# A second kernel's tail woven with gathers: 1.8 instead of 1.2 rows' weight for a turn of attention, 1.0 instead of 1.1 elsewhere, and the small diagonals made on VectorE

## The chip, the cores and the metric

One core of a Trainium2 chip runs the whole program. The metric is the device time in microseconds of one execution, as the median of three runs. The engines are TensorE (PE; its weight loads are PEld), VectorE (DVE), ScalarE (ACT), GpSimd (POOL) and SyncE (SP), which issues the loads of the weights.

## The reference

Two blocks work on 512 tokens of 1024 channels in fp32. The first ends in a mixture of 16384 experts: every token takes 8 x 16 = 128 of them, each with a row `u` and a row `v` of 1024 numbers.

```
ue = take(expert_u, expert);  ve = take(expert_v, expert)
h  = gelu(einsum('thkd,td->thk', ue, xc))
out = einsum('thk,thkd->td', gate * h, ve)
```

The second block is attention with 8 heads (two softmaxes a head, "diff"), an MLP of width 4096 with squared relu, a second attention with 8 heads ("mla"), a second MLP, and a norm. Both attentions are causal, so the first 256 tokens can pass through the whole second block before the last 256 are known.

## The kernel before

**The rows.** An expert's `u` and `v` lie together (8 KB). What the code calls row `n` is one of 512 gathers: GpSimd issues an indirect DMA that brings 128 experts' pairs, one to a partition, 1 MB in all (L1754). VectorE multiplies the `u` half with the token and sums (the dot, L1892), ScalarE makes the gelu (L1847), multiplies it with the gate (L1849) and makes a diagonal matrix of the 128 results (L1856 or L1859), and TensorE adds diagonal times `v` into PSUM (L1778 or L1782). Rows 0 to 255 belong to tokens 0 to 255. From row 256 on a row is "stacked": it holds 32 experts for each of four tokens, its diagonal is 128x32 (`each32` is four 32x32 identities), and its product is 4 matmuls. The rows lie in a ring: 6 buffers from row 236 and 7 from row 278 on. GpSimd issues the gather of row n when TensorE is done with row n-7.

**The tail.** From row 256 on, the second block for tokens 0 to 255 (`halves[0]`) runs with the remaining rows. Each engine's program is written as generators that yield once a turn; `beside` adds `rate * weight` for each yield and takes one step of the row generator whenever the sum passes 1. The same turns are counted on PE, ACT and DVE, so their orders agree. A turn in a projection or an MLP's first product is 24 matmuls of 128x256 (weight 1), in an MLP's second product 12 (weight 0.5). A turn of attention (19 turns for the 16 blocks of 128 queries, since it is pipelined over four) makes the scores of block n, the softmax of n-1, the transposes of n-2 and the product with v of n-3. In turn order, ACT does exp for block n, then two copies for older blocks, and then the row's gelu. In one step of a row, DVE makes the dot of row n+1, and PE, one step behind (`LAG`), adds row n-1.

**The weights.** A tile is 512 KB of fp32. SP loads it, ACT rounds it to a high part (`act_hi`, L297), and GpSimd makes the low part (`pool_lo`, L303), in program order between the gathers. ACT does `act_hi` of a later tile right after TensorE has finished the one in its slot. PSUM has 8 banks, 4 of which are for the tail while rows run beside it; so the scores of the next block wait for the exp of the one before.

After the last row the second half of the tokens (`halves[1]`) passes through the same code alone.

Of the kernel before, what the change touches and what calls it, by code (L numbers as in the profile page):

```python
# [11 lines left out]
ALU = mybir.AluOpType  # L12
ACT = mybir.ActivationFunctionType
# [4 lines left out]
NEG = -1.0e30  # L18
NBANK = 8
FEW_ROWS = 236  # L20
RATE = 1.1
SEVEN_ROWS = 278
LAG = 1
COLS = 53120
# [168 lines left out]
class Net:  # L193
# [1227 lines left out]
    def with_rows(self, rest, choose, regroup, rows, tail):  # L1421
# [7 lines left out]
        self.banks, self.nbank = 4, 0  # L1429
        self.beside(tail(self.halves[0]), rows, RATE)  # L1430
        for _ in rows:
# [330 lines left out]
    def pe_rows(self, e):  # L1762
        S, D_, A_ = "peer_pe", "peer_dve", "peer_act"
        for step in range(-1, 512 + LAG):
            if step < 511 and self.stacked(step + 1) and (step + 1) % 32 == 0:
                self.pe_repeat(e, step + 1)
            n = self.late(step)
            if n is not None:
                tt, k, row = n // 128, n % 128, self.rows[self.row_of(n)]
                b = 4 if tt == 0 else 6  # L1770
                if k == 0 and tt >= 2:
                    e.wait_ge(*self.at(A_, ("sums", tt - 1)))
                e.wait_ge(*self.at(A_, ("diag", n)))
                if self.stacked(n):
                    g = k // 32
                    for c in range(4):
                        o = self.ps[32 * c:32 * c + 32, b + g // 2, 256 * (g % 2):256 * (g % 2) + 256]
                        ins = e.matmul(o, self.diag[1][n % 4][:, 0:32], row[:, 1024 + 256 * c:1280 + 256 * c],  # L1778
                                       start=k % 32 == 0, stop=k % 32 == 31)
                else:  # L1780
                    for half in range(2):
                        ins = e.matmul(self.ps[:, b + half, :], self.diag[n >= 128][n % 4],  # L1782
                                       row[:, 1024 + 512 * half:1536 + 512 * half], start=k == 0, stop=k == 127)
                ins.then_inc(*self.tick(S, ("acc", n)))
                self.spot[("row", n)] = self.turn
            if step in (130, 386 + LAG):
                self.pe_join(e, step // 128 - 1)
            yield
# [53 lines left out]
    def act_weight(self, e, n):  # L1842

        S, c, k = "peer_act", slice(n % 128, n % 128 + 1), n % 128
        dots, gelus, weight = self.dots[n >= 128], self.gelus[n >= 128], self.weight[n >= 128]
        e.wait_ge(*self.at("peer_dve", ("dot", n)))
        e.activation(gelus[:, c], dots[:, c], ACT.Gelu, bias=0.0, scale=1.0).then_inc(*self.tick(S))  # L1847
        e.wait_ge(*self.last(S))
        e.activation(weight[:, c], gelus[:, c], ACT.Identity, bias=0.0,  # L1849
                     scale=self.gate[n // 128][:, k:k + 1]).then_inc(*self.tick(S, ("weight", n)))  # L1850
        if n >= 4:
            e.wait_ge(*self.at("peer_pe", ("acc", n - 4)))
        e.wait_ge(*self.at(S, ("weight", n)))
        diag = self.diag[n >= 128][n % 4]
        if self.stacked(n):
            e.activation(diag[:, 0:32], self.each32, ACT.Identity, bias=0.0,  # L1856
                         scale=weight[:, c]).then_inc(*self.tick(S, ("diag", n)))
        else:
            e.activation(diag, self.C("ident"), ACT.Identity, bias=0.0,  # L1859
                         scale=weight[:, c]).then_inc(*self.tick(S, ("diag", n)))  # L1860

    def act_join(self, e, tt):
        b = 4 if tt == 0 else 6
# [5 lines left out]
    def dve_rows(self, e):  # L1869
        S, A_, P_ = "peer_dve", "peer_act", "peer_pe"  # L1870
        for n in range(-1, 512 + LAG):
            if n + 1 < 512:
                self.dve_dot(e, n + 1)
            if n in (130, 386 + LAG):
                for j in range(8):
                    self.dve_join(e, n // 128 - 1, j)
            yield

    def dve_dot(self, e, n):
        S, r = "peer_dve", self.row_of(n)  # L1880
        if n in (0, 128):
            e.wait_ge(*self.at("peer_act", ("xn", 0 if n == 0 else 3, 1)))
        if n == 129:
            e.wait_ge(*self.at("peer_pe", ("acc", 127)))
        if n:
            e.wait_ge(*self.at(S, ("dot", n - 2 if 129 < n < 256 else n - 1)))
        xn = self.XN[:, n // 128, :]
        if self.stacked(n):
            e.wait_ge(*self.at("peer_pe", ("repeated", n - n % 32)))
            xn = self.xn_bank()  # L1890
        e.wait_ge(*self.at(f"row{r}", n))
        e.scalar_tensor_tensor(out=self.junk[0 if n < 128 else n % 2 if n < 256 else 1], in0=self.rows[r][:, 0:1024], scalar=1.0, in1=xn,  # L1892
                               op0=ALU.mult, op1=ALU.mult,
                               accum_out=self.dots[n >= 128][:, n % 128:n % 128 + 1]).then_inc(*self.tick(S, ("dot", n)))
# [280 lines left out]
    def attention(self, H, scores, softmaxed, turn, meet):  # L2175
        blocks = [(hh, qb) for hh in range(8) for qb in (2 * H.h, 2 * H.h + 1)]
        for n in range(len(blocks) + 3):
            if n < 16:
                scores(n, *blocks[n])
            if 1 <= n <= 16:  # L2180
                softmaxed(n - 1, *blocks[n - 1])
            if 2 <= n <= 17:
                turn(n - 2, *blocks[n - 2])
            if n >= 3:
                meet(n - 3, *blocks[n - 3])
            yield 1.2

    @staticmethod
    def nothing(n, hh, qb):
# [1011 lines left out]
```

## Time and profile before

| what | value |
|---|---|
| median of 3 runs | 3049.65 us (3047.44 to 3058.9) |
| the profiled execution: its time, its span | 3047.7 us, 3045.9 us |
| PE busy | 2585.2 us (85%) |
| DVE busy | 1763.8 us (58%) |
| ACT busy | 1388.3 us (46%) |
| POOL busy | 1648.2 us (54%) |
| DMA, mean | 262 GB/s |

The span is the time from the first to the last instruction; 1.8 us lie around it. Busy shares are means over stages with different limits. The stretch which the change concerns goes from the first stacked row at 1287 us to the last at 2310 us. In it lie the projections (to 1409), the first attention (to 1510), its output product (to 1561), the first MLP (to 1833), projections (to 1917), the second attention (to 2013), its output product (to 2057) and the second MLP (to 2310).

### The profile page before, as it was taken

To read this page: it belongs to the slowest core of one execution; us is meant where nothing else is said; L and a number is where in the kernel's file an instruction comes from. 1 tells how busy PE (TensorE), PEld (TensorE's weight loads), DVE (VectorE), ACT (ScalarE), POOL (GpSimd) and SP (SyncE) were. 2 spreads that over 40 slices of the span, in tenths; PEclk is the share of its full clock that TensorE was granted. 3 is DMA by queue.
4 is the path that set the end of the run, shared out by engine and by line. 5 is a ranking of instruction groups with operands and counts; after the bars stand their busy time and mean duration, and the time that the engine had idled before them with its cause. 6 is when DMAs were issued, how large, how long until landed. Compare 5 with 4: busy or idle time off the path is not lost. (4 is left out here: it accounts for less than half of the span.)

```text
span 3045.9 us, 49365 instructions
## 1 busy us (share of the span) xinstructions
PE 2585.2 (85%) x18974; PEld 1960.1 (64%) x18974; DVE 1763.8 (58%) x3863; ACT 1388.3 (46%) x3129; POOL 1648.2 (54%) x973
## 2 busy tenths in 40 slices
PE   6997977987877777687698997679997999999998
PEld 3865965743333232265477776458776979989998
DVE  5686433767777776765654457565446463256323
ACT  2231222243344343456865456765554454444543
POOL 3822113834444443466287776358883618852785
PEclk8988978999999999888799998889997999999999
DMA  7210013289999999779789997989995415542453
GB/s 293 101 59 26 4 57 152 93 331 421 421 421 421 421 421 415 316 300 401 284 325 401 377 389 296 376 314 393 402 409 218 152 34 175 187 134 74 157 186 115
DMA packets 140538, 797.61 MB, mean 262 GB/s; under 512 B 15504, under 2 KB 18704, under 8 KB 67600
## 3 DMA queue, kind: packets, MB, share of 16 engines
q0 software_dynamic: 73728, 536.90, 43.4%
q1 hardware_dynamic: 65856, 253.09, 23.3%
q10 hardware_dynamic: 720, 4.46, 0.3%
q8 instruction: 151, 2.47, 0.3%
q14 instruction: 83, 0.68, 0.1%
HBM read 787.84 MB, written 6.55 MB: 261 GB/s over the span
## 5 line engine op out<-in xcount | busy, mean ns | idle before, releaser
L303 POOL TENSOR_TENSOR wls<-raws,whs 128x1024 fp32r<-128x1024 f32 (+1 forms) x256 | 612.0, 2400 | 370.3 <-ACT whs L297 368.3
L1998 PE MATMUL ps<-ts,whs 128*128 128x256 f32 x1424 | 292.2, 306 | 27.5 <-DVE ts L2093 19.6
L1754 POOL DMA_INDIRECT raw<-in_peer_uv,un x205 | 209.3, 1021 | 191.7 <-PE ps L1778 87.6
L297 ACT CAST whs<-raws 128x1024 fp32r<-128x1024 f32 (+1 forms) x256 | 263.9, 1036 | 96.8 <-PE ps L2576 35.2
L303 POOL TENSOR_TENSOR wlw<-raws,whw 128x1024 fp32r<-128x1024 f32 x112 | 267.8, 2404 | 70.4 <-ACT whw L297 69.7
L1847 ACT ACTIVATE un<-un 128x1 f32<-128x1 f32 x384 | 77.6, 202 | 445.6 <-DVE scratch L1892 432.0
L1998 PEld LDWEIGHTS ps<-ts,whs 128*128 128x128 f32 x1424 | 239.6, 205 | 56.1 <-issue 26.8
L1892 DVE SCALAR_TENSOR_TENSOR scratch<-raw,ps 128x1024 f32<-128x1024 f32 x149 | 181.4, 1217 | 133.4 <-DMA raw<-in_peer_uv,un 120.2
L2576 PE MATMUL ps<-ts,whs 128*128 128x256 f32 x1216 | 228.7, 289 | 0.2 <-DVE ts L2629 0.2
L1998 PE MATMUL ps<-ts,wls 128*128 128x256 f32 x712 | 209.8, 295 | 0.0
L303 POOL TENSOR_TENSOR wl<-raw,wh 128x2048 fp32r<-128x2048 f32 x23 | 107.1, 4660 | 186.0 <-ACT wh L297 186.0
L2576 PEld LDWEIGHTS ps<-ts,whs 128*128 128x128 f32 x1216 | 190.6, 193 | 19.8 <-issue 16.8
L2557 PE MATMUL ps<-ts,whs 128*128 128x256 f32 x1088 | 202.3, 287 | 0.0
L2557 PE MATMUL ps<-ts,whw 128*128 128x256 f32 x960 | 182.6, 291 | 9.5 <-DVE ts L2093 9.5
L2658 DVE TENSOR_TENSOR kept<-kept,ps 128x256 f32<-128x256 f32 x256 | 103.8, 418 | 129.4 <-PE ps L2576 129.3
L2557 PEld LDWEIGHTS ps<-ts,whs 128*128 128x128 f32 x1088 | 170.3, 193 | 12.8 <-issue 11.9
L2576 PE MATMUL ps<-ts,wls 128*128 128x256 f32 x608 | 172.8, 284 | 0.0
L2557 PEld LDWEIGHTS ps<-ts,whw 128*128 128x128 f32 x960 | 152.5, 195 | 22.2 <-DVE ts L2093 10.7
L1892 DVE SCALAR_TENSOR_TENSOR scratch<-raw,scratch 128x1024 f32<-128x1024 f32 x108 | 135.6, 1260 | 50.4 <-DMA raw<-in_peer_uv,un 26.1
L1754 POOL DMA_INDIRECT un<-in_peer_uv,un x104 | 105.2, 1011 | 108.7 <-PE ps L1782 51.6
L333 PE MATMUL ps<-uh,wh 128*128 128x512 f32 x368 | 149.3, 406 | 15.3 <-DVE ul L1281 5.3
L2622 DVE SCALAR_TENSOR_TENSOR ps<-ps,rs 128x256 f32<-128x256 f32 x128 | 55.2, 431 | 179.2 <-PE ps L2557 178.9
(443 smaller groups left out, 6883.2 us busy)
## 6 DMA issues: line engine op xcount, KB each, us to landing
raws<-in_w_up SPq DMA_DIRECT2D x128, 512.0 KB, 4.2
raws<-in_w_down SPq DMA_DIRECT2D x128, 512.0 KB, 4.7
scratch<-in_ada_w SPq DMA_DIRECT2D x17, 1024.0 KB, 13.2
raws<-in_w_qk SPq DMA_DIRECT2D x32, 512.0 KB, 8.5
raw<-in_w_in SPq DMA_DIRECT2D x11, 1024.0 KB, 5.3
raw<-in_peer_w_q SPq DMA_DIRECT2D x8, 1024.0 KB, 8.0
raws<-in_w_v SPq DMA_DIRECT2D x16, 512.0 KB, 5.7
raws<-in_w_o_a SPq DMA_DIRECT2D x16, 512.0 KB, 4.0
```

The source lines that it names most:

```text
L297: e.copy(self.wh[h][:, 0:width], self.raw[slot][:, 0:width]).then_inc(*self.tick("hi", key))
L303: e.tensor_tensor(self.wl[h][:, 0:width], self.raw[slot][:, 0:width], self.wh[h][:, 0:width].bitcast(F32), ALU.subtract).then_inc(*self.ti ...
L333: ins = e.matmul(self.ps[:, b, :], l, r, start=k == 0 and i == 0, stop=k == nk - 1 and i == 2)
L1754: e.indirect_dma_start(self.rows[r], None, self.d["peer_uv"], index).then_inc(*self.tick(f"row{r}", n, 16))
L1847: e.activation(gelus[:, c], dots[:, c], ACT.Gelu, bias=0.0, scale=1.0).then_inc(*self.tick(S))
L1892: e.scalar_tensor_tensor(out=self.junk[0 if n < 128 else n % 2 if n < 256 else 1], in0=self.rows[r][:, 0:1024], scalar=1.0, in1=xn, op0=AL ...
L1998: ins = e.matmul(o[:, 0:256], l, r, start=k == 0 and i == 0, stop=k == nk - 1 and i == 2)
L2557: ins = e.matmul(o[:, 0:256], l, r, start=k == 0 and n == 0, stop=k == 7 and n == 2)
L2576: ins = e.matmul(o[:, 0:256], l, r, start=t == 0 and n == 0, stop=t == 3 and n == 2)
L2622: e.scalar_tensor_tensor(out=x, in0=x, scalar=0.0, in1=H.rs, op0=ALU.max, op1=ALU.mult).then_inc(*self.tick(S, ("ready", g, t)))
L2658: e.tensor_tensor(x, x, self.bh((P_, "v", g, j)), ALU.add).then_inc(*self.tick(S, ("x", g, j)))
```

## The change

`RATE` goes from 1.1 to 1.0, and a turn of attention has weight 1.8 instead of 1.2. For a stacked row, ScalarE makes only the gelu. VectorE makes the diagonal in one `tensor_scalar` with two factors, gelu and gate, and does it after the dot of the next row. TensorE waits for VectorE's tick in place of ScalarE's.

```diff
-RATE = 1.1
+RATE = 1.0
...
-                e.wait_ge(*self.at(A_, ("diag", n)))
+                e.wait_ge(*self.at(D_ if self.stacked(n) else A_, ("diag", n)))
...
         e.wait_ge(*self.at("peer_dve", ("dot", n)))
+        if self.stacked(n):
+            e.activation(gelus[:, c], dots[:, c], ACT.Gelu, bias=0.0, scale=1.0).then_inc(*self.tick(S, ("gelu", n)))
+            return
...
             if n + 1 < 512:
                 self.dve_dot(e, n + 1)
+            if 0 <= n < 512 and self.stacked(n):
+                self.dve_diagonal(e, n)
...
+    def dve_diagonal(self, e, n):
+
+        k = n % 128
+        e.wait_ge(*self.at("peer_act", ("gelu", n)))
+        e.wait_ge(*self.at("peer_pe", ("acc", n - 4)))
+        e.tensor_scalar(self.diag[1][n % 4][:, 0:32], self.each32, self.gelus[1][:, k:k + 1], self.gate[n // 128][:, k:k + 1],
+                        ALU.mult, ALU.mult).then_inc(*self.tick("peer_dve", ("diag", n)))
...
-            yield 1.2
+            yield 1.8
```

How the 257 steps of rows in this stretch are dealt, counted in the two programs:

| stage | turns | steps before | steps after |
|---|---|---|---|
| join | 1 | 3 | 3 |
| projections of diff | 24 | 26 | 24 |
| attention diff (19 turns), and one turn of weight 2 | 20 | 27 | 36 |
| its output product | 8 | 9 | 8 |
| first MLP | 96 | 71 | 64 |
| projections of mla | 29 | 17 | 15 |
| attention mla | 19 | 25 | 34 |
| its output product | 8 | 9 | 8 |
| second MLP | 96 | 70 | 64 |
| final norm | 2 | 0 | 1 |

In an attention 6 of the 19 turns had two steps and 13 had one; now 15 have two and 4 have one.

**VectorE, a turn of the second attention.** Before, block 137's turn: the maximum of the scores (L2939), its scaling, the softmax of the block before (L2946, L2948), the low part of an older block (L2954), and here two dots (L1892).

```order
L2939 TENSOR_REDUCE kept<-ps 128x1
L2941 TENSOR_SCALAR kept<-kept 128x1
L2946 RECIPROCAL kept<-kept 128x1
L2948 TENSOR_SCALAR me_137<-me_137,kept 128x128
L2954 TENSOR_TENSOR ts_90<-ps,ts_90 128x128
L1892 SCALAR_TENSOR_TENSOR scratch,un<-scratch,ps 128x1024
L1892 SCALAR_TENSOR_TENSOR scratch,un<-un,ps 128x1024
```

After, the same turn (lines moved by 8): each dot is followed by the diagonal of the row before it (L1884).

```order
L2947 TENSOR_REDUCE kept<-ps 128x1
L2949 TENSOR_SCALAR kept<-kept 128x1
L2954 RECIPROCAL kept<-kept 128x1
L2956 TENSOR_SCALAR me_137<-me_137,kept 128x128
L2962 TENSOR_TENSOR ts_90<-ps,ts_90 128x128
L1900 SCALAR_TENSOR_TENSOR scratch,un<-raw_64,ps 128x1024
L1884 TENSOR_SCALAR un<-kept,un 128x32
L1900 SCALAR_TENSOR_TENSOR scratch,un<-raw_65,ps 128x1024
L1884 TENSOR_SCALAR un<-kept,un 128x32
```

So the first of the two diagonals stands between the dots, and the second stands ahead of the next block's maximum.

**ScalarE, between two exps of the second attention.** Before, with two rows:

```order
L2827 ACTIVATE me_136,kept<-ps,kept 128x256
L2206 COPY mat_134<-ps 128x256
L2837 CAST ts_90<-ps 128x128
L1847 ACT_TABLE_LOAD
L1847 ACTIVATE un<-un 128x1
L1849 ACTIVATE un<-un 128x1
L1856 ACTIVATE un<-kept,un 128x32
L1847 ACTIVATE un<-un 128x1
L1849 ACTIVATE un<-un 128x1
L1856 ACTIVATE un<-kept,un 128x32
L2827 ACT_TABLE_LOAD
```

After:

```order
L2835 ACTIVATE me_136,kept<-ps,kept 128x256
L2214 COPY mat_134<-ps 128x256
L2845 CAST ts_90<-ps 128x128
L1848 ACT_TABLE_LOAD
L1848 ACTIVATE un<-un 128x1 x2
L2835 ACT_TABLE_LOAD
```

Four instructions are gone; both table loads stay.

**TensorE, a turn of the second attention.** Before, the turn which scores a block of 128 keys (L2720 to L2722), turns one (L2201), multiplies one with v (L2215) and adds one row (L1778), and then the next scores:

```order
L2720 MATMUL ps<-kn_117,qn_124 128x128
L2721 MATMUL ps<-kr_119,qr_125 128x128
L2722 MATMUL ps<-kept 128x128
L2201 MATMUL ps<-kept,me_135 128x128
L2215 MATMUL ps<-mat_134,vm_118 128x128 x2
L1778 MATMUL ps<-raw_67,un 32x256 x4
L2720 MATMUL ps<-kn_117,qn_124 128x256
```

After, two rows stand between the same scores:

```order
L2728 MATMUL ps<-kn_117,qn_124 128x128
L2729 MATMUL ps<-kr_119,qr_125 128x128
L2730 MATMUL ps<-kept 128x128
L2209 MATMUL ps<-kept,me_135 128x128
L2223 MATMUL ps<-mat_134,vm_118 128x128 x2
L1778 MATMUL ps<-raw_67,un 32x256 x4
L1778 MATMUL ps<-scratch,un 32x256 x4
L2728 MATMUL ps<-kn_117,qn_124 128x256
```

The second of them needs the diagonal that VectorE makes between the two dots of the same turn.

## Rows read from the trace of the kernel before

**Rows 1.** The page: GB/s in 40 slices, the gathers' queue, two costly groups

```profile
GB/s 293 101 59 26 4 57 152 93 331 421 421 421 421 421 421 415 316 300 401 284 325 401 377 389 296 376 314 393 402 409 218 152 34 175 187 134 74 157 186 115
q0 software_dynamic: 73728, 536.90, 43.4%
L303 POOL TENSOR_TENSOR wls<-raws,whs 128x1024 fp32r<-128x1024 f32 (+1 forms) x256 | 612.0, 2400 | 370.3 <-ACT whs L297 368.3
```

**Rows 2.** Windows by stage: length, busy PE, PEld, DVE, ACT, POOL, PEclk, DMA share, GB/s

```profile
1318.00:1377.00 59.00, 59.00 (x488) 47.40 (x487) 37.40 (x80) 30.44 (x74) 45.98 (x28) 0.98 0.89 352
1409.00:1510.00 101.00, 64.86 (x436) 36.51 (x432) 66.03 (x202) 87.85 (x221) 32.02 (x31) 0.73 0.84 324
1561.00:1833.00 272.00, 253.31 (x2158) 206.96 (x2157) 142.21 (x293) 146.18 (x357) 206.51 (x127) 0.96 0.95 377
1917.00:2013.00 96.00, 61.92 (x392) 37.08 (x384) 45.89 (x129) 76.67 (x172) 31.24 (x30) 0.73 0.88 337
2057.00:2310.00 253.00, 240.41 (x2095) 198.90 (x2094) 130.28 (x265) 135.79 (x335) 201.26 (x123) 0.99 0.97 391
```

**Rows 3.** Timeline of ScalarE, second attention: start us, us, instruction

```profile
1947.22 0.37 ACT L2827 ACTIVATE me<-ps,kept 128x128 f32<-128x128 f32 x1
...
1949.49 0.20 ACT L1847 ACTIVATE un<-un 128x1 f32<-128x1 f32 x1 [0.19 <-DVE scratch L1892]
1949.73 0.29 ACT L1849 ACTIVATE un<-un 128x1 f32<-128x1 f32 x1
1950.12 0.32 ACT L1856 ACTIVATE un<-kept,un 128x32 f32<-128x32 f32 x1
1950.45 1.28 ACT L2827 ACT_TABLE_LOAD   x1
1951.75 0.47 ACT L2827 ACTIVATE me<-ps,kept 128x256 f32<-128x256 f32 x1
...
1955.50 0.20 ACT L1847 ACTIVATE un<-un 128x1 f32<-128x1 f32 x1 [0.32 <-DVE scratch L1892]
...
1956.46 1.28 ACT L2827 ACT_TABLE_LOAD   x1
1957.76 0.37 ACT L2827 ACTIVATE me<-ps,kept 128x128 f32<-128x128 f32 x1
```

**Rows 4.** Timeline of VectorE and TensorE around the same turns

```profile
1945.58 1.22 PE L2720 MATMUL ps<-kn,qn 128*128 128x256 f32 x2
...
1952.98 1.21 DVE L1892 SCALAR_TENSOR_TENSOR scratch<-raw,ps 128x1024 f32<-128x1024 f32 x1
...
1954.24 1.22 DVE L1892 SCALAR_TENSOR_TENSOR scratch<-scratch,ps 128x1024 f32<-128x1024 f32 x1
...
1955.96 0.70 PE L2720 MATMUL ps<-kn,qn 128*128 128x256 f32 x2
```

**Rows 5.** Timeline of the second MLP: one row's step and the next dot

```profile
2148.81 1.22 DVE L1892 SCALAR_TENSOR_TENSOR scratch<-raw,ps 128x1024 f32<-128x1024 f32 x1 [1.86 <-DMA raw<-in_peer_uv,un]
...
2150.70 0.32 ACT L1856 ACTIVATE un<-kept,un 128x32 f32<-128x32 f32 x1
...
2151.07 0.64 PE L1778 MATMUL ps<-raw,un 128*32 128x256 f32 x8
...
2152.58 1.22 DVE L1892 SCALAR_TENSOR_TENSOR scratch<-raw,ps 128x1024 f32<-128x1024 f32 x1 [1.88 <-DMA raw<-in_peer_uv,un]
```

**Rows 6.** Waits in the second MLP: who waited for whom, us, times, longest

```profile
DVE scratch L1892 <- DMA raw<-in_peer_uv,un: 44.6, 28, 2.6
...
POOL wls L303 <- ACT whs L297: 27.7, 15, 9.0
```

**Rows 7.** Timeline of VectorE and GpSimd at another diagonal (L2048)

```profile
2341.50 0.48 DVE L2048 TENSOR_SCALAR diag<-kept 128x128 f32<-128x128 f32 x2
...
2344.46 4.65 POOL L303 TENSOR_TENSOR wls<-raws,whs 128x1024 fp32r<-128x1024 f32 x2 [26.64 <-ACT whs L297]
...
2345.83 3.36 DVE L2048 TENSOR_SCALAR diag<-kept 128x128 f32<-128x128 f32 x2
```

**Rows 8.** The line L2048: its duration, shortest, median, longest, in ns

```profile
L2048 DVE TENSOR_SCALAR diag<-kept x8: 273/674/2374, 1311.3 to 2346.8; 128x128 f32<-128x128 f32 x8
```

More of the change, by code:

```diff
@@ L1853, in act_weight @@
         e.wait_ge(*self.at(S, ("weight", n)))
[L1854 to L1860, printed above, removed]
+        e.activation(self.diag[n >= 128][n % 4], self.C("ident"), ACT.Identity, bias=0.0,
+                     scale=weight[:, c]).then_inc(*self.tick(S, ("diag", n)))
     def act_join(self, e, tt):
```

## The prediction

> **What bounds the kernel now.** I read the page first, then the busy time by stage, then inside two stages the timeline and the waits. The page says that from 690 us on the chip's memory is read at up to 421 GB/s for long stretches, and that the gathers are 536.90 MB in 512 rows, so 1.05 MB a row [rows 1]. At 421 GB/s a row costs 2.5 us of transfer and a 512 KB weight tile 1.25 us. These two prices carry most of what follows.
>
> The busy times by stage [rows 2] show three kinds of stage. In the two MLPs the DMA share is 0.95 and 0.97 at 377 and 391 GB/s. Their 64 turns' weight bring 64 tiles and 71 or 70 rows: 64 x 1.25 + 70 x 2.5 = 255 us, beside the 253 us that the second takes and the 272 us of the first. They are bound by transfer; the waits agree, since the dot waits for landings, 44.6 us for one kind of buffer alone [rows 6]. TensorE is close behind with 240.41 us of 253, so nobody is far from the edge. In the first projections TensorE is busy 59.00 of 59.00 us while the DMA share is 0.89: bound by TensorE. In the two attentions neither is full. The first has ScalarE busy 87.85 us of 101, the second 76.67 of 96; DMA moves 324 and 337 GB/s, and TensorE's granted clock is 0.73 of full, so that it stood at 1.2 GHz for about half of the time.
>
> Inside the second attention the exps tell a turn's length [rows 3]: 1947.22 to 1951.75 is 4.53 us with one row, 1951.75 to 1957.76 is 6.01 us with two. The turn is a circle: exp, two copies, table load, dot, gelu, gate, diagonal, table load, exp. A row more costs 1.5 us of it.
>
> So the change takes 13 rows out of the MLPs, where each is 2.5 us of the bound resource, and 6 out of the projections and products, gives one to the final norm, and puts 9 into each attention, where there is transfer to spare.
>
> **The change part by part.**
>
> *MLPs.* 6 rows fewer in the second and 7 in the first: 13 x 2.5 = 32.5 us less transfer. The next limit is TensorE: 240.41 minus 6 x 0.6 us [rows 2, 5] leaves about 237 us for the second, so 253 - 15 = 238 is just allowed. The first has 272 - 17.5 = 254.5 above 253.31 - 7 x 0.6 = 249. Bounds: no less than 13 x 0.6 = 8 us saved if only TensorE's part came out, no more than 32.5.
>
> *The diagonal in the MLPs.* ScalarE loses two instructions a row, but it is busy 135.79 of 253 us there, and its own loss is nothing. The wait moves: TensorE now adds row n only after the dot of row n+1. In [rows 5] the dot starts at 2148.81 and TensorE adds the row at 2151.07; the next dot starts 3.77 us after the first, waiting 1.88 us for its landing. So TensorE falls back by one row's pace, up to 3.8 us, once for each stretch that is paced by landings; it had run one turn ahead of VectorE and ScalarE, and this lead is what covers it. I cost it at nothing. If the lead were gone, scores, exp and rounding behind TensorE would slip once by 3.8 us a stage. What recurs is VectorE's own new instruction. Its nearest row is L2048, also constant times per-partition factor, four times as wide: two took 0.48 us with GpSimd idle, and 3.36 us when GpSimd had begun `pool_lo` at 2344.46 [rows 7]; the line runs from 273 to 2374 ns [rows 8]. I take 0.2 us where GpSimd is idle or gathers (bounds 0 and 0.28). During a `pool_lo` it waits for what is left of 2.40 us [rows 1], 1.2 on average and 2.4 at most. 64 such instructions in 253 us are 0.61 of the time, so the mean is 0.7 us a row, 0 to 2.4 for one. VectorE is busy 130.28 us of 253 and waits for landings, so most of this falls into its idle time. From the end of a TensorE turn VectorE needs about 0.85 us for the tail's two instructions, 1.26 for the dot and 0.2 for the diagonal, 2.3 us, and TensorE asks for the diagonal 3.45 us after (a row's 0.57 and 24 matmuls' 2.9). A hold above 1.15 us is therefore a stall: its mean over a hold spread evenly to 2.4 us is 0.33 us, times 0.61 is 0.2 us a turn, 64 turns, 12.5 us an MLP at most, and half or less of it where landings set the pace anyway. I give back 8.5 us for both. MLPs together: -24.
>
> The Trainium skill, page "SBUF — State Buffer", section "Who interferes with whom", says that GpSimd and VectorE share a port pair by an exclusive lock, that an fp32 `tensor_scalar` with source and destination in SBUF can take it, and that whoever comes second blocks for the whole instruction. The trace agrees: the same line takes 0.27 us or 2.37 us. By the rule every diagonal pays it; by the row for a narrower one it could also be free, and the MLPs would then gain the whole 32.5 us.
>
> *Attentions.* ScalarE's 0.75 us (1949.73 to the table load at 1950.45) goes from each turn's circle, so one row makes 3.8 us. With two rows the second gelu starts 0.2 us later for the diagonal between the dots and the table load follows it: 6.01 - 0.76 + 0.2 = 5.45 us. But TensorE closes a second circle. Its second row of a turn needs the first diagonal, which follows the first dot: in the turn of 1951.75 the dots start at 1952.98 and 1954.24 [rows 4], the diagonal would be there at 1954.4, 2.65 us after the exp. Then come the row (0.6 us), the next scores (about 1.3 us), maximum and scaling (0.55), the exp: 5.3 us, no longer than ScalarE's circle. At 1.2 GHz the first score product takes 1.22 us instead of 0.70 [rows 4], the row about 1.1, the scores 2 to 2.9: 6.5 us. With the clock as now, 0.46 of the time at full speed, a two-row turn is 6.0. Of the 16 turns with an exp 12 will have two rows and 4 one: 12 x 6.0 + 4 x 3.8 = 87 us. Now it is 5 x 5.9 + 11 x 4.6 = 80. The last three turns gain one row, 1.4 us. Second attention: +8 us, with bounds +1 (all at full clock) and +15 (all at 1.2 GHz). GpSimd has few `pool_lo` here (31.24 us busy), so the hold is left out. In the first attention ScalarE is closer to being the whole circle, its relief counts more, and I take +4, bounds -4 and +15. Transfer allows it: 36 rows x 2.5 = 90 us beside some 9 tiles, 11 us, in 105 us. That is tight, and what speaks against a shorter attention.
>
> *Other stages.* Six rows fewer. In the projections TensorE is the bound and two rows are 1.2 us; elsewhere a row is between 0.6 and 2.5 us. I take -6 for all six and give 2 back for held diagonals: -4. The last row now ends after the sums of the final norm; the norm's own chain on VectorE is longer, nothing.
>
> *Sum.* +8 + 4 - 24 - 4 = -16 us. Against the profiled execution's 3047.7 us this is 3031.7. That execution lies 2 us below the median of 3049.65, so I name 3033 for the median.
>
> **The rivals.**
>
> *The forecast*, the MLPs gain most of their transfer and the attentions pay half of it back: 0.40, 3022 to 3044.
>
> *Attentions take the rows for nothing.* More rows keep TensorE at full clock, two-row turns are 5.4 us, holds hide: 0 in the attentions, -32.5 in the MLPs, -6 elsewhere: 3047.7 - 38.5 = 3009. For it: ScalarE at 87.85 of 101 is the plain bound now and loses 0.75 us a turn. Against it: TensorE still waits in every turn. 0.22.
>
> *The rows cost in the attentions what they save elsewhere.* Two-row turns of 6.5 us, or landings that come too late at 1.8 rows a turn: +15 and +13, -24, -4, so 3048. For it: the granted clock of 0.73, and 101 us of transfer to be done in 105. 0.22.
>
> *Held diagonals make it slower.* TensorE, VectorE and GpSimd form one circle: held diagonal, late row, late turn, late rounding by ScalarE, and GpSimd, which already waits 27.7 us for that [rows 6], issues the gathers later. 128 rows run in the MLPs and some 50 in projections and products. Without any hold the change would save 38.5 us there and pay 12 in the attentions; so it decides from 26.5 / 178 = 0.15 us a row that comes onto the path, where I counted 10.5 / 178 = 0.06. At 0.3 us a row it is 53 - 26.5, +27: 3075. Against it: VectorE waits about 1.9 us ahead of a dot. 0.16.
>
> **How the numbers follow.** A measurement of this kernel can tell about 0.5%, 15 us, from no change. Faster by more: the second case and somewhat over half of the forecast's, 0.46. Within: the rest of the forecast's and the third, 0.37. Slower: the fourth, 0.17, with a little of the third. The range of 8 in 10 leaves out most of the last case and the end of the second: 3006 to 3062. The likeliest case alone is 3022 to 3044.
>
> **What would show it.** In the profile after: the stage times, MLPs near 260 and 241 us at unchanged or higher GB/s, attentions near 105 and 104; exps 3.8 and 5.4 to 6.5 us apart, and TensorE's scores waiting for the diagonal in the long ones; the new instruction 0.2 us in the attentions and spread up to 2.4 us in the MLPs; ScalarE's time in the second attention down by about 15 us for diagonals and gates. The prediction is wrong if the MLPs do not get shorter with fewer rows, which would say that the circle and not transfer set them, or if TensorE's waits for the diagonal grow from a few us to tens in an MLP.

## The result, and the profile after

The changed kernel takes 3073.13 us (median of 6 runs, 3065.62 to 3081.19) against 3051.32 us for the kernel before in the same comparison: ratio 1.0075, 95% interval 1.0056 to 1.0093. It is slower by about 22 us. I had forecast 3033 us.

In what follows a stage runs from TensorE's first instruction of it to that of the next, but an MLP ends with its last product: what lies between that and the next stage (0.5 us before, 5.7 us after the change, at the end of the first MLP) is in the line below it. By these bounds the first attention of the kernel before lasts to 1521 us and its second output product to 2050 us, where I had put 1510 and 2057 ahead of the prediction. Each column is one profiled execution; the last two are kernels of the experiments below.

| stage | before | after | dealing alone | PSUM source |
|---|---|---|---|---|
| ahead of the projections | 1301.9 | 1303.7 | 1308.0 | 1306.5 |
| projections of diff | 107.3 | 107.2 | 104.7 | 106.2 |
| attention diff | 112.2 | 128.6 | 127.2 | 125.6 |
| its output product | 40.2 | 42.3 | 38.1 | 41.3 |
| first MLP | 270.5 | 245.2 | 247.7 | 242.9 |
| projections of mla | 85.0 | 89.3 | 82.8 | 84.7 |
| attention mla | 96.1 | 118.0 | 106.7 | 117.6 |
| its output product | 36.3 | 41.2 | 39.5 | 38.5 |
| second MLP | 260.1 | 265.8 | 244.9 | 242.0 |
| the second half, alone | 736.2 | 730.4 | 740.0 | 735.1 |
| span | 3045.9 | 3071.6 | 3039.7 | 3040.5 |

The change leaves the second half alone and touches three rows ahead of the projections, and these two lines still move by 10 and 6 us between kernels; a single stage is read to a few us, no better. Against before, the first MLP gained 25 us (20 if the 5.7 us behind it are counted), more than forecast, and the rest lost it again: the attentions +16 and +22, the second MLP +6 although it has six rows fewer, the small stages +11.

The page of the changed kernel: GB/s in 40 slices, the new group, and TensorE's rows with what they waited for.

```profile
GB/s 294 98 68 17 4 56 151 113 334 421 422 421 416 421 416 399 312 315 379 355 274 413 415 364 287 341 330 365 359 376 242 153 18 186 177 142 79 152 187 116
L1884 DVE TENSOR_SCALAR un<-kept,un 128x32 f32<-128x32 f32 x256 | 209.3, 818 | 3.1 <-ACT un L1848 2.8
L1778 PE MATMUL ps<-raw,un 128*32 128x256 f32 x1192 | 109.6, 444 | 93.5 <-DVE un L1884 80.5
```

The new instruction has a mean of 818 ns, four times what I had taken for an undisturbed one. In the slices of the second MLP, the 28th to 30th, 365, 359 and 376 GB/s stand where 393, 402 and 409 stood [rows 1]. Busy times by stage, first of before at the boundaries of the table (columns as in [rows 2]):

```profile
1409.30:1521.40 112.10, 73.57 (x468) 41.64 (x464) 72.58 (x215) 92.92 (x232) 33.60 (x33) 0.74 0.86 333
1561.70:1832.20 270.50, 251.81 (x2146) 206.38 (x2146) 140.91 (x291) 145.08 (x354) 205.71 (x127) 0.96 0.95 377
1917.00:2013.30 96.30, 62.22 (x392) 37.08 (x385) 46.19 (x129) 76.67 (x172) 31.47 (x30) 0.73 0.88 337
2049.60:2309.70 260.10, 244.80 (x2130) 202.59 (x2130) 136.49 (x273) 140.40 (x345) 205.21 (x126) 0.99 0.98 392
```

and of after:

```profile
1410.90:1539.50 128.60, 89.90 (x541) 47.29 (x537) 91.74 (x267) 75.89 (x181) 38.36 (x40) 0.67 0.92 356
1581.70:1826.90 245.20, 237.72 (x2086) 199.44 (x2082) 183.21 (x335) 98.90 (x203) 202.41 (x123) 1.00 0.97 391
1916.20:2034.20 118.00, 72.98 (x461) 41.02 (x457) 66.04 (x183) 62.53 (x130) 34.19 (x35) 0.70 0.85 323
2075.40:2341.10 265.70, 244.79 (x2070) 206.01 (x2066) 175.30 (x326) 95.66 (x197) 198.22 (x120) 0.96 0.92 353
```

The first MLP is at a DMA share of 0.97 with TensorE busy 237.72 of 245 us, so it is at both bounds. The second attention and the second MLP moved less per second than before (323 and 353 GB/s); neither transfer nor any engine fills them, so a wait does. ScalarE is relieved of 14 us in the second attention, and the stage is 22 us longer.

**The wait in the second attention.** Waits there (who waited for whom, us, times, longest):

```profile
POOL raw L1754 <- PE ps L1778: 46.9, 20, 6.9
PE ps L1778 <- DVE un L1884: 44.2, 20, 3.9
```

The timeline of one turn with two rows, from exp to exp:

```profile
1960.48 0.37 ACT L2835 ACTIVATE me<-ps,kept 128x128 f32<-128x128 f32 x1
...
1961.50 1.21 DVE L1900 SCALAR_TENSOR_TENSOR scratch<-un,ps 128x1024 f32<-128x1024 f32 x1
...
1962.64 0.30 DVE L1884 TENSOR_SCALAR un<-kept,un 128x32 f32<-128x32 f32 x1
...
1962.99 1.08 PE L1778 MATMUL ps<-scratch,un 128*32 128x256 f32 x8 [2.98 <-DVE un L1884]
...
1964.00 1.22 PE L2728 MATMUL ps<-kn,qn 128*128 128x256 f32 x2
...
1966.55 0.42 DVE L2947 TENSOR_REDUCE kept<-ps 128x1 f32<-128x256 f32 x1 [2.26 <-PE ps L2730]
...
1967.23 1.28 ACT L2835 ACT_TABLE_LOAD   x1 [2.93 <-DVE kept L2954]
...
1968.53 0.47 ACT L2835 ACTIVATE me<-ps,kept 128x256 f32<-128x256 f32 x1
```

Between the exp and the dot lie the copies and the low part of older blocks. From the dot on, every instruction shown starts when the one above it is done: start of the exp to end of the diagonal 2.46 us, the row 1.06, the scores at 1.2 GHz 2.55, maximum and scaling 0.68, the table load 1.30, sum 8.05 us. ScalarE waits 2.93 us ahead of the table load, so the load comes after the wait. From exp to exp the 12 two-row turns of this attention take 7.45 us in the mean, the 3 others 4.39.

**The wait in the second MLP.** Waits there:

```profile
ACT ps L2614 <- DVE ps L2630: 83.2, 31, 5.0
...
POOL wls L303 <- ACT whs L297: 33.5, 14, 11.1
...
PE ps L1778 <- DVE un L1884: 20.9, 7, 3.5
```

Before, the dots waited for landings in this stage, 44.6 us for one kind of buffer [rows 6]; the same wait is 1.9 us now. One of TensorE's seven waits in the timeline:

```profile
2266.26 0.95 POOL L1754 DMA_INDIRECT raw<-in_peer_uv,un  x1
2266.90 0.09 DVE L1900 DVE_READ_ACCUMULATOR scratch<-scratch,ps 128x1 f32 x1
2266.90 5.05 DVE L1884 TENSOR_SCALAR un<-kept,un 128x32 f32<-128x32 f32 x1
2267.18 0.20 ACT L1848 ACTIVATE un<-un 128x1 f32<-128x1 f32 x1
2267.24 2.38 POOL L303 TENSOR_TENSOR wlw<-raws,whw 128x1024 fp32r<-128x1024 f32 x1
2269.57 2.34 POOL L303 TENSOR_TENSOR wls<-raws,whs 128x1024 fp32r<-128x1024 f32 x1
...
2272.01 0.64 PE L1778 MATMUL ps<-raw,un 128*32 128x256 f32 x8 [3.32 <-DVE un L1884]
```

The diagonal is held through two `pool_lo` in a row, 5.05 us, and TensorE stands 3.32 us. This happens six times, at 2128, 2162, 2196, 2232, 2266 and 2300 us, with waits of 3.3 to 3.5 us: 20 of the 20.9. The granted clock falls behind it (columns as above):

```profile
2265.00:2268.69 3.69, 3.69 (x33) 3.07 (x32) 3.60 (x5) 1.79 (x4) 3.52 (x3) 1.00 1.00 409
2268.69:2272.01 3.32, 0.00 (x1) 0.00 (x1) 3.32 (x2) 0.00 (x0) 3.21 (x2) 1.00 1.02 406
2272.01:2276.19 4.18, 4.18 (x27) 3.77 (x28) 1.96 (x5) 1.79 (x4) 3.02 (x2) 0.63 0.97 364
```

In 4.18 us after the stall TensorE did 27 matmuls, where 3.69 us ahead of it had held 33: most of this stretch was at 1.2 GHz, and the stretch ahead of the stall was at 2.4.

### The profile page after: what moved, and what is told of

Its sections match the earlier page's. It is cut to its first block, busy times and chain, and to the rows that moved or that the text cites. A ratio compares the mean times of both kernels' runs of the same rounds, so it can differ in the third digit from the quotient of the medians.

```text
span 3071.6 us, 49109 instructions
## 1 busy us (share of the span) xinstructions
PE 2606.4 (85%) x18974; PEld 1966.8 (64%) x18974; DVE 1941.9 (63%) x4119; ACT 1233.9 (40%) x2617; POOL 1645.0 (54%) x973
## 4 chain that ended last, share of the span: by engine, by line
PE 51%; DVE 17%; DMA 14%; issue 4%; ACT 3%; POOL 3%; DVEq 0%; SPq 0%; ACTq 0%
PE ps L2584 11%; PE ps L2565 10%; PE ps L2006 7%; PE ps L1782 4%; DMA raw<-in_peer_uv,un 4%; PE ps L872 4%; DVE scratch L1900 3%; PE ps L1778 3%; PE ps L333 3%; DMA un<-in_peer_uv,un 3%; DMA raw<-in_peer_uv,scratch 3%; DVE un L1884 2%; DMA w<-in_peer_uv,scratch 2%; POOL wls L303 1%; DMA w<-in_peer_uv,un 1%
## 5 line engine op out<-in xcount | busy, mean ns | idle before, releaser
L1754 POOL DMA_INDIRECT raw<-in_peer_uv,un x205 | 202.8, 989 | 208.8 <-PE ps L1778 103.8
L297 ACT CAST whs<-raws 128x1024 fp32r<-128x1024 f32 (+1 forms) x256 | 263.9, 1037 | 98.9 <-PE ps L2006 38.5
L1884 DVE TENSOR_SCALAR un<-kept,un 128x32 f32<-128x32 f32 x256 | 209.3, 818 | 3.1 <-ACT un L1848 2.8
L1778 PE MATMUL ps<-raw,un 128*32 128x256 f32 x1192 | 109.6, 444 | 93.5 <-DVE un L1884 80.5
L1848 ACT ACTIVATE un<-un 128x1 f32<-128x1 f32 x256 | 50.8, 202 | 288.4 <-DVE scratch L1900 275.0
L1900 DVE SCALAR_TENSOR_TENSOR scratch<-raw,scratch 128x1024 f32<-128x1024 f32 x108 | 135.3, 1260 | 48.7 <-DMA raw<-in_peer_uv,un 23.4
L1754 POOL DMA_INDIRECT un<-in_peer_uv,un x104 | 105.6, 1015 | 111.6 <-PE ps L1778 50.4
```

The lines of the kernel that those rows point to most:

```text
L297: e.copy(self.wh[h][:, 0:width], self.raw[slot][:, 0:width]).then_inc(*self.tick("hi", key))
L1754: e.indirect_dma_start(self.rows[r], None, self.d["peer_uv"], index).then_inc(*self.tick(f"row{r}", n, 16))
L1884: e.tensor_scalar(self.diag[1][n % 4][:, 0:32], self.each32, self.gelus[1][:, k:k + 1], self.gate[n // 128][:, k:k + 1], ALU.mult, ALU.mul ...
```

## The experiments

All ran in three groups; each ratio is against runs of the kernel before in the same group. I turn a ratio into us with 3051. The theory at the outset: the dealing gains, and VectorE's diagonal loses more, by its place in the attentions and by its holds in the MLPs. The chief rival: rows cost in the attentions, whoever makes the diagonal.

**1. The dealing alone.**

```diff
-RATE = 1.1
+RATE = 1.0
...
-            yield 1.2
+            yield 1.8
```

> Only the dealing of the changed kernel (1.0 and 1.8 rows' weight); ScalarE makes gate and diagonals as before. Theory (the place of the diagonal and its holds make the loss, the dealing gains): two-row turns stay near 6.0 us in both attentions, each attention is 8 to 12 us longer than before, the first MLP near 245 us as in the changed kernel (it was bound by landings before, 270 us) and the second near 245; about 3030 us. Rival (rows dealt to an attention cost there, whoever makes the diagonal, since TensorE falls to 1.2 GHz): attentions 20 us or more longer each, two-row turns 7 us, 3060 us or more.

Measured 3036.77 us, ratio 0.9949 (0.9930 to 0.9968), -16 us. Busy times of both attentions and the second MLP:

```profile
1412.70:1539.90 127.20, 83.24 (x540) 45.68 (x536) 83.11 (x233) 100.14 (x260) 39.59 (x41) 0.71 0.94 366
...
1908.50:2015.20 106.70, 69.84 (x461) 38.54 (x457) 59.14 (x147) 84.10 (x200) 38.95 (x39) 0.75 0.97 376
...
2054.70:2299.60 244.90, 238.21 (x2070) 200.28 (x2066) 127.57 (x261) 133.00 (x322) 196.30 (x118) 0.99 0.97 388
```

The theory's sum holds. The attentions cost 15.0 and 10.6 us more with ScalarE's diagonals too, where the theory had 8 to 12. The rival's long turns are not there: the median of the two-row turns, from exp to exp, is 5.98 and 5.90 us in the two attentions, against 5.98 and 6.01 before. There are 12 of them instead of 5, and this makes most of the price: from the first exp to the last the attentions take 92.1 and 89.8 us instead of 83.1 and 79.6. The DMA shares of 0.94 and 0.97 say that little more could be moved, but landings are not what these stages wait for: the dots waited for them 17.8 and 11.1 us in sum, against 13.6 and 9.0 before. The other 7 us of the first attention lie behind its last exp (28.2 us instead of 21.2).

**2. The diagonals alone**, with 1.1 and 1.2 as before.

> Only the diagonals on VectorE; the dealing as before (1.1 and 1.2). Theory: 5 two-row turns an attention get 1.4 us longer and 10 one-row turns 0.7 us shorter, so the attentions change by under 3 us each; the second MLP keeps some waits of TensorE for held diagonals, 10 to 20 us, partly beside waits for landings: 3050 to 3065 us. Rival (the dealing alone makes the loss): 3051 us or less, no wait for the diagonal over 5 us in sum in an MLP. Rival (held diagonals make all of it): 3075 us, since more rows lie in the MLPs.

Measured 3076.18 us, ratio 1.0083 (1.0063 to 1.0104), +25 us. That is the number of the second rival, held diagonals, and above the theory's range; the rival of the dealing falls. But the second rival's reason is not met, since the MLPs are not where the loss is. The attentions take 101.6 and 90.5 us, 11 and 6 less than before: there the relief of ScalarE is real when most turns have one row (4.69 and 4.19 us for such a turn, against 5.13 and 4.53). The loss lies outside: first projections 121.4 us against 107.3, the others and the products +8, +5 and +9, second MLP +5. In the projections the waits for the diagonal are few and long, and the clock is 0.90 where it is 0.95 in the change and 0.96 with the dealing alone:

```profile
1307.20:1428.70 121.50, 108.06 (x836) 89.12 (x836) 82.49 (x155) 39.62 (x76) 80.38 (x49) 0.90 0.82 310
```

```profile
PE ps L1778 <- DVE un L1884: 8.7, 3, 3.1
```

**3. The diagonal ahead of the dot.**

```diff
-            if n + 1 < 512:
-                self.dve_dot(e, n + 1)
             if 0 <= n < 512 and self.stacked(n):
                 self.dve_diagonal(e, n)
+            if n + 1 < 512:
+                self.dve_dot(e, n + 1)
```

> The changed kernel, with the diagonal of row n ahead of the dot of row n+1 in VectorE's step instead of behind it. Theory (the dot lies on the circle of a two-row turn): two-row turns 1.2 us shorter, 24 of them, so the attentions together 25 to 30 us shorter, and some holds in the MLPs keep their price: 3040 to 3055 us. Rival (the holds or the slow clock make the attentions long): attentions unchanged, 3068 to 3078 us.

Measured 3054.30 us, ratio 1.0018 (1.0006 to 1.0031), 17 us better than the change. The total fits, its parts don't: the attentions gained 0 and 6 us, not 25 to 30, and 13.5 us came from the second MLP, which I had not expected. Two-row turns of the second attention went from 7.45 to 6.72 us; VectorE now waits for gelu, so part of what the dot gave is lost. In the second MLP:

```profile
2064.90:2317.20 252.30, 237.61 (x2070) 199.43 (x2066) 212.73 (x326) 99.05 (x197) 199.48 (x119) 0.99 0.95 375
```

```profile
PE ps L1778 <- DVE un L1884: 10.9, 9, 1.3
```

VectorE is busy 212.73 us instead of 175.30, so the diagonals were held longer in sum, and TensorE waited half as long: a hold costs by when it falls, not by its length.

**4. A diagonal that GpSimd does not hold.**

```diff
-        e.tensor_scalar(self.diag[1][n % 4][:, 0:32], self.each32, self.gelus[1][:, k:k + 1], self.gate[n // 128][:, k:k + 1],
-                        ALU.mult, ALU.mult)
+        e.scalar_tensor_tensor(out=self.diag[1][n % 4][:, 0:32], in0=self.each32, scalar=self.gelus[1][:, k:k + 1],
+                               in1=self.xn_bank()[:, 0:32], op0=ALU.mult, op1=ALU.mult)
```

TensorE's copy of the next tokens into that bank now waits for the diagonal of row n-2 instead of the dot of row n-1.

> The changed kernel, with a diagonal of the same size and place that reads PSUM as second source (a scalar_tensor_tensor of the four identities, the gelu, and 32 columns of the token's copy in PSUM instead of the gate, which is left out, so the output differs). In the trace of before an operation with a source in PSUM is never held by GpSimd. Theory: the six holds of 5 us in the second MLP go, with 20 us of TensorE's waits and some of the lower clock, the second MLP takes about 243 us instead of 266, the attentions stay at 135 and 121: 3045 to 3053 us. Rival (held diagonals explain all of the loss): 3030 us or less. Rival (the waits in the MLP come from the order, diagonal behind the dot, not from the hold): second MLP stays at 260 or more.

Measured 3035.78 us, ratio 0.9947 (0.9927 to 0.9967), -16 us against before and 39 us better than the change, more than the theory had and between it and its first rival. The second MLP takes 244.2 us, as expected; the rest came in the first attention (-8), the mla projections (-5) and the two products (-5). All 256 diagonals took the same time (ns, shortest, median, longest):

```profile
L1884 DVE SCALAR_TENSOR_TENSOR un<-kept,un,ps x256: 234/244/248, 1298.8 to 2299.2; 128x32 f32<-128x32 f32 x128
```

Against it the second MLP of the changed kernel:

```profile
L1884 DVE TENSOR_SCALAR un<-kept,un x64: 289/298/5247, 2076.1 to 2337.2; 128x32 f32<-128x32 f32 x64
```

The Trainium skill, page "SBUF — State Buffer", section "Who interferes with whom", says that a VectorE instruction with at most one input in SBUF, outside the modes that use both ports, does not contend with GpSimd. The trace agrees, 248 ns at most.

The instruction has changed with its source, so the form could be the cure. Traces on record say that it is not. The dot of the kernel before is a scalar_tensor_tensor too. With its second source in SBUF, up to row 255, it could be held; with the source in PSUM none of 256 took over 1.23 us. And the kernel of number 8 has another scalar_tensor_tensor with both sources in SBUF, which was held (one line from each of the two runs):

```profile
L1892 DVE SCALAR_TENSOR_TENSOR scratch<-raw,scratch x108: 1203/1224/3361, 611.7 to 1273.7; 128x1024 f32<-128x1024 f32 x108
L2104 DVE SCALAR_TENSOR_TENSOR ts<-kept,ts x64: 471/480/2571, 1292.0 to 2839.5; 128x256 fp32r<-128x256 f32 x64
```

**5. TensorE two steps behind.**

```diff
-LAG = 1
+LAG = 2
```

> The changed kernel with TensorE two steps behind instead of one. Theory (in a two-row turn TensorE's second row needs a diagonal that VectorE makes behind the first dot of the same turn, and the scores, the maximum and the table load follow it): with the diagonal of the turn before, two-row turns of the second attention fall from 7.45 to about 6 us, 12 of them, 15 us; a hold of 5 us finds one row more of lead and its 20 us of waits in the second MLP halve: 3035 to 3050 us. Rival (the lead is paid by the ring: buffers come free one row later, so landings come late): the dots wait for landings over 40 us in an attention or an MLP, 3065 us or more.

Measured 3081.55 us, ratio 1.0088 (1.0073 to 1.0102). The theory was right in the attention and the rival in the MLPs, and the total is the rival's. First MLP, second attention, second MLP:

```profile
1575.70:1850.60 274.90, 252.46 (x2090) 208.01 (x2090) 177.59 (x345) 103.75 (x211) 206.24 (x125) 0.94 0.92 358
1932.30:2036.70 104.40, 70.58 (x461) 38.30 (x457) 67.11 (x179) 62.62 (x129) 38.54 (x38) 0.74 0.96 374
2076.60:2349.30 272.70, 250.33 (x2067) 211.06 (x2066) 185.52 (x324) 96.33 (x195) 196.53 (x119) 0.94 0.91 350
```

The attention falls from 118.0 to 104.4 us, ten of its twelve two-row turns lie between 4.98 and 6.39 us (median 5.73, against 7.65 in the change): the diagonal's place set the long turn. The MLPs grow by 30 and 7 us, as the rival said: in the second the dots wait again for landings, 33.8 and 24.3 us for two kinds of buffer, and weight loads 23.4 us for diagonals.

**6 and 7. VectorE's diagonals by stage.** A function `on_dve(n)` picks the rows; the others are ScalarE's as before.

```diff
+    def on_dve(self, n):
+        return 283 <= n < 319 or 406 <= n < 440
```

In the second of the two it returns the other stacked rows.

> The changed kernel, with VectorE's diagonals only for the rows dealt to the two attentions (70 of 256), ScalarE's elsewhere. Theory (outside the attentions VectorE's diagonal costs by holds, inside by its place): attentions as in the changed kernel, 129 and 118 us, all other stages as with the dealing alone, so 3036.8 + 2 + 11 = 3050 us. Rival (the diagonals in the attentions only look long because gathers and weights come late from the stage before): second attention 107 us, 3038 us.

> The complement: VectorE's diagonals for all stacked rows but those of the attentions. Theory: attentions as with the dealing alone (127 and 107 us), the second MLP 266 us and the projections and products as in the changed kernel: 3060 us. Rival (the diagonals in the attentions make the loss): 3040 us, second MLP 250 or less.

Measured 3050.57 us, ratio 0.9993 (0.9982 to 1.0005), and 3057.24 us, ratio 1.0024 (1.0008 to 1.0041). Above the dealing alone these are +13 and +23 us; together 36, and the whole change is 38 above it, so the two prices add up within the intervals, which are 4 to 6 us to either side. The second attention takes 117.9 us with VectorE's diagonals and 102.2 with ScalarE's, the second MLP 247.3 and 265.6:

```profile
2055.80:2321.40 265.60, 244.89 (x2070) 206.03 (x2066) 175.43 (x326) 95.69 (x197) 198.28 (x120) 0.96 0.92 354
```

The first attention is 125.0 and 125.9: there it makes no difference.

**8. The PSUM source with the gate.** ScalarE makes gelu and gate, and VectorE's second source is bypassed.

```diff
+        e.scalar_tensor_tensor(out=self.diag[1][n % 4][:, 0:32], in0=self.each32, scalar=self.weight[1][:, k:k + 1],
+                               in1=self.xn_bank()[:, 0:32], op0=ALU.mult, op1=ALU.bypass)
```

> The changed kernel with the same output, and a diagonal that reads PSUM: ScalarE makes gelu and gate, VectorE multiplies the identities with the result by a scalar_tensor_tensor whose second source, in PSUM, is bypassed. Theory (the hold falls on a VectorE instruction whose sources both lie in SBUF): as in the kernel without the gate, second MLP 244, attentions about 121 us, ScalarE's 0.3 us a row more on the attention's circle: 3034 to 3044 us. Rival (a bypassed source isn't read and the instruction is held all the same): second MLP 260 or more, 3065 to 3075 us.

Measured 3042.27 us, ratio 0.9967 (0.9954 to 0.9980).

```profile
L1887 DVE SCALAR_TENSOR_TENSOR un<-kept,un,ps x256: 235/243/248, 1303.4 to 2305.4; 128x32 f32<-128x32 f32 x128
```

```profile
1907.20:2024.80 117.60, 68.93 (x460) 39.92 (x456) 62.59 (x182) 73.21 (x166) 38.55 (x39) 0.74 0.89 333
2063.30:2305.30 242.00, 236.14 (x2070) 198.35 (x2066) 138.08 (x327) 116.34 (x262) 199.16 (x120) 1.00 0.97 391
```

The second MLP is 24 us shorter than in the change. The edit also moves the gate to ScalarE and makes TensorE's copy of the tokens wait for a diagonal, and both can only add work or waits. The second attention stays at 117.6 us: what it loses has nothing to do with holds.

**9 and 10. Less and more dealing**, diagonals on ScalarE: 1.047 and 1.5, 0.947 and 2.2.

> The kernel before with half of the dealing: 1.047 and 1.5 rows' weight, diagonals on ScalarE; 67 rows in each MLP, some 30 in each attention. Theory (an MLP is bound by landings down to about 245 us, an attention pays a fixed price for each turn with two rows): the gain of the full dealing, 14.6 us, comes about half: 3040 to 3048 us. Rival (the price of the attentions comes only with the last rows, when landings run short there): 3030 us or less.

> The dealing carried further: 0.947 and 2.2 rows' weight, diagonals on ScalarE; 61 and 60 rows in the MLPs, some 40 in each attention. Theory (in the MLPs TensorE is next to bind, 235 to 240 us, so that little is left to gain, and 40 rows of transfer are over 100 us in an attention): MLPs 240 to 245 us each, attentions 135 and 120 us, 3040 to 3055 us. Rival (transfer alone sets the MLPs): MLPs 238 or less, attentions unchanged, 3025 us or less.

Measured 3043.81 us, ratio 0.9988 (0.9975 to 1.0001), and 3036.81 us, ratio 0.9968 (0.9953 to 0.9983); the first can't be told from the kernel before, and the second is a little better than I expected. Sums of both MLPs and of both attentions: before 530.6 and 208.3 us; at 1.5 513.3 and 226.4; at 1.8 492.6 and 233.9; at 2.2 482.4 and 257.2. The MLPs have 134, 128 and 121 rows instead of 141 and get 2.4 to 2.9 us shorter for each row fewer. Past 1.8 they still give 10 us, and the attentions pay 23 for it. The two-row turns stay where they were: medians of 5.98 and 6.01 us at 1.5, of 5.98 and 5.80 at 2.2.

**11. Both prices avoided:** the new dealing, ScalarE's diagonals in the attentions, VectorE's with the PSUM source elsewhere.

> The new dealing, ScalarE's diagonals for the rows of the attentions, and VectorE's diagonals with a bypassed source in PSUM for all others. Theory (both prices of the diagonals avoided): MLPs 243 and 242 us as in the kernel with the PSUM source, attentions 126 and 105 us as with ScalarE: 3024 to 3034 us. Rival (ScalarE's relief outside the attentions is worth nothing, since landings pace the MLPs): as with the dealing alone, 3035 to 3038 us.

Measured 3027.12 us, ratio 0.9926 (0.9909 to 0.9943): the fastest here, 23 us below the kernel before. Its attentions take 125.7 and 107.1 us, its MLPs 241.9 and 243.7, as forecast. It is ahead of the dealing alone, of another group, by 0.23%, and the intervals overlap; that part is not shown.

**12. The PSUM source with the diagonal first.**

> The kernel with the PSUM source (3042.3 us), with the diagonal ahead of the next row's dot in VectorE's step. Theory (dot on the circle of a two-row turn): two-row turns of the second attention 0.6 to 0.9 us shorter, 12 of them, the attention about 110 us instead of 118, the MLPs unchanged: 3032 to 3038 us. Rival (without holds the order no longer matters, or VectorE's wait for gelu and gate costs as much): 3040 to 3045 us.

Measured 3064.61 us, ratio 1.0049 (1.0031 to 1.0067), 25 us worse than without the new order, where I had expected 4 to 10 better. Its waits, over the whole span:

```profile
DVE un L1887 <- ACT un L1850: 62.6, 64, 3.3
```

```profile
PE ps L1778 <- DVE un L1887: 102.0, 46, 11.2
...
PE ps L1800 <- DVE un L1887: 19.9, 7, 8.7
```

In this order the diagonal must wait for gelu and gate of the row whose dot has just ended, and the next dot stands behind it; in number 3 that wait was 22.8 us in the stacked rows, for gelu alone. The 19.9 us come from the copy of the tokens, which now waits for the diagonal of row n-1. By stage, most of the loss is in the first attention, 136.0 us instead of 125.6, and the MLPs are 5 and 4 us longer; the second attention is 2.7 us shorter. So the same order that helped where diagonals could be held cost here, where none was (249 ns at most). How much of the 25 us is which of the two waits I did not separate.

## Why the prediction was wrong

*The MLPs, -24.* Near as a sum (-25.3 and +5.7, -19.6) and wrong in how, so that the nearness is chance. Freed of the diagonal, they give 22.8 and 15.2 us for 7 and 6 rows (dealing alone), a little over the 32.5 us of transfer that I had counted, and TensorE is next as I said (238.21 busy of 244.90). With VectorE's diagonals the first kept its gain, and the second gave all of it back and 6 us more.

*A diagonal held, "0 to 2.4" us, 0.06 us a row on the path.* This step failed. Undisturbed the diagonal takes 0.30 us, where I had 0.2, and a hold can last two `pool_lo`, 5.05 us. The reckoning with a mean over a hold spread evenly was wrong as well: in the first MLP 26 holds of 1.0 to 2.5 us cost little (TensorE waited 6.5 us in sum), in the second six of them cost 3.3 us of standing each and the clock behind it: TensorE's busy time is 244.79 us there and 238.21 with the dealing alone. The PSUM source is worth 1.0075 - 0.9967 = 1.1%, 33 us, 0.13 us for each of 256 rows. The rival with held diagonals named this loss, and I gave it 0.16. That its 3075 us is so near the 3073 measured is luck: it had 0.3 us a row on the path of 178 rows, 53 us, against a saving of 26.5 without holds, and number 8 shows 33 us against a saving of 10.

*The attentions, +8 and +4.* This is the term that was furthest off: +21.9 and +16.4, 26 us more. It has two parts, and in each a step of mine failed.

First, the rows themselves. With the dealing alone the attentions are 15.0 and 10.6 us longer: of the +38, 26 are this. My reckoning of turns, without any relief of ScalarE, gives it for the second: 12 x 6.0 + 4 x 4.6 = 90 against 80, +10. What failed is the relief that I then took off, down to +8 and +4: the first attention, where "its relief counts more", is 16 us longer and not 4. Its one-row turns did get shorter (4.11 us instead of 5.13), but only 3 are left. Its first four two-row turns take 6.9 to 9.5 us, at a DMA share of 1.01 and 0.98, and what lies behind its last exp takes 32.2 us instead of 21.2. Transfer is a floor and not the cause of most of it. The queues' work of before, 0.86 of 112.1 and 0.88 of 96.3 us, is 96 and 85 us, and nine rows more make 119 and 107, beside 127 and 107 measured. That looks like the bound, but at a weight of 1.5 (number 9), with five rows more, the same sum is 109 and 97 us, and the attentions took 123.4 and 103.1. Only at 2.2, with 15 rows more, does it come near in both: 134 and 122 against 136.5 and 120.7.

Second, the circle of a two-row turn, in the second attention. I had it as 5.3 us, "no longer than ScalarE's", 6.5 at 1.2 GHz and 6.0 in the mean (its terms, 2.65, 0.6, 1.3 and 0.55, add up to 5.1). The steps were the right ones, with one missing: ScalarE's table load, 1.28 us, comes only after the maximum. With it the turn is 8.05 us at 1.2 GHz, and 7.45 in the mean. Twelve turns at 1.45 us more are 17 us, more than the 14 that the stage is off by. TensorE two steps behind, or ScalarE's diagonals, bring the median back to 5.7 and 5.9 us. One-row turns were forecast at 3.8 and took 4.39 here. In the first attention the two-row turns have a mean of 6.63 and a median of 6.17 us; the dealing alone has 6.46 and 5.98 there, so the missing step costs little in it.

*Other stages, -4.* They are +11. With the dealing alone they are -2.6, -2.1, -2.2 and +3.2, sum -3.7; VectorE's diagonals add 15 us to them, where I had given back 2 for holds.

*Moving TensorE's row behind the next dot "costs nothing".* True in the MLPs without holds (242.9 and 242.0 us), false where two rows share a turn of the second attention.

*Added up,* the change is the dealing, -16 us, and VectorE's diagonals, +38. Of these 33 us go with the hold. The place costs 11 us in the second attention, half of which the relieved ScalarE seems to return elsewhere, as the MLPs of number 8 are 3 to 5 us shorter than with the dealing alone. The third of my cases had +15 and +13 us in the attentions, by two-row turns of 6.5 us or by late landings. The dealing alone gives +15.0 and +10.6, by more two-row turns and not by longer ones, so its numbers were right and its reasons were not. Open is what makes the first attention so long behind its last exp; it is so with either engine, 28.2 us with ScalarE's diagonals and 32.2 with VectorE's.

## What to carry to other kernels

Before work is dealt to a stage that looks idle, make two sums. Its DMA share times its length, with the transfers that come with the work, is a floor. The turns, each at the length that a turn with so much work has now, are the other. Here the floor lay 14 and 6 us too low at a weight of 1.5, and the turns told the price of the second attention. When an instruction moves to another engine, write out the whole circle from one repeated instruction to its next self, table loads included. And give a VectorE instruction that others wait for one source in PSUM when GpSimd works on SBUF beside it: 244 ns each time instead of 0.3 to 5.2 us.

## What the runs showed of the hardware that was not expected

**A gather's issue holds a diagonal too, and a hold can go on into the next instruction.** The six diagonals of 5.05 to 5.25 us began 0.33 to 0.52 us ahead of the first `pool_lo`. But GpSimd was already issuing a gather (L1754), begun 0.44 to 0.64 us before the diagonal. Such an issue can hold a diagonal by itself. Ten others of the changed kernel began with 0.42 to 0.52 us of an issue left, and they took 0.43 to 0.53 us, to its end:

```profile
1464.38 0.94 POOL L1754 DMA_INDIRECT raw<-in_peer_uv,un  x1 [2.13 <-PE ps L1778]
...
1464.79 0.53 DVE L1884 TENSOR_SCALAR un<-kept,un 128x32 f32<-128x32 f32 x1 [0.28 <-ACT un L1848]
```

The 13 that began with 0.56 us or more left took 0.3 us. That is no fixed bound: in number 5 three that began with 0.60 to 0.75 us left, and a `pool_lo` 0.02 us behind the issue, were held for 3.1 to 3.2 us. The next `pool_lo` then decides. Of the diagonals that began with 0.30 to 0.32 us of an issue left, twelve took 0.30 us, and in these `pool_lo` began 0.14 or 0.15 us after the issue's end; five took 5.05 us, and in these it began 0.01 to 0.02 us after it. The sixth long one began with 0.51 us left. Why these six were not let through between the two `pool_lo`, as six others were that met such a pair (at 1753 us, for one, after 2.42 us), stays open.

The Trainium skill, page "SBUF — State Buffer", section "Who interferes with whom", says that whoever issues first gets the shared ports for the whole instruction and the other blocks. With the gather's issue counted as GpSimd's first instruction the trace agrees. What it adds is that the one held can stay held over three instructions in a row. Starts that lie closer than about 0.1 us do not tell who was first: four diagonals that began 0.04 to 0.08 us ahead of a `pool_lo`, with no gather before it, were held for 2.4 to 2.5 us.

A scalar_tensor_tensor whose second source in PSUM is bypassed takes as long as one that uses it, 243 against 244 ns, and is not held either.
